# Reordering ScalarE's and VectorE's work between projection and prompt attention, and the last sums and transposes, in a one-layer hybrid decoder step

## The reference

```python
h = rms_norm(x, prm['ln_mix'])
q, kv_c, kv_s, kv_w, gates, z, xbc, dt_raw = split_projection(h, prm['w_in'])
o_cmp, p_cmp = compressed_attention(q, compress_kv(kv_c, *cmp_params(prm)), qpos)
idx = select_blocks(p_cmp, qpos, -(-T // SEL_BLOCK))
# o_sel: attention over the selected blocks; o_win: sliding window of 512
attn = gate_branches(gates, o_cmp, o_sel, o_win)
ssd_y, conv_new, ssm_new = mamba2_mixer(z, xbc, dt_raw, ...)
# finish_layer
x = x + jnp.concatenate([attn, ssd_y], axis=-1) @ prm['w_out']
h = rms_norm(x, prm['ln_mlp'])
x = x + jnp.square(jax.nn.relu(h @ prm['w_up'])) @ prm['w_down']
# at the end
y_prompt = rms_norm(hp, ln_final); y_sample = rms_norm(hs, ln_final)
```

## Time and profile before

| | us |
|---|---|
| median of 3 runs | 2792.65 |
| lowest and highest run | 2785.09, 2793.06 |
| profiled execution, its own time | 2792.96 |
| its span, first to last instruction | 2791.2 |
| TensorE busy in the span | 2647.1 |
| VectorE busy | 1137.0 |
| ScalarE busy | 843.3 |
| mean granted TensorE clock | 0.973 of full speed |

### The profile page before, as it was taken

One profiled execution on the slowest core, in us unless ns is written; L12 is line 12 of the kernel. 1 busy time (PEld: TensorE's weight loads), 2 busy tenths in 40 slices (PEclk: granted clock), 3 DMA queues, 4 the chain that ended last, 5 costly groups with the idle time before them and its releaser, 6 DMA issues.

```text
span 2791.2 us, 50988 instructions
## 1 busy us (share of the span) xinstructions
PE 2647.1 (95%) x21237; PEld 2533.8 (91%) x21237; DVE 1137.0 (41%) x1710; ACT 843.3 (30%) x1360; POOL 107.3 (4%) x116
## 2 busy tenths in 40 slices
PE   7889999999699788999999999999999999999998
PEld 6779999998577557998999999999999999999998
DVE  4432224554676578433333333333333233333333
ACT  3242112223565345322212212222122122221233
POOL 0000000000000041110000000000000000000011
PEclk9999999999799888999999999999999999999999
DMA  5145333233002744322323222222222222222222
GB/s 214 61 159 161 95 93 90 73 101 101 3 31 100 213 128 136 98 91 76 94 89 95 90 90 90 90 90 90 93 95 90 90 90 90 90 90 92 95 90 86
DMA packets 241815, 274.64 MB, mean 98 GB/s; under 512 B 19397, under 2 KB 233811, under 8 KB 237494
## 3 DMA queue, kind: packets, MB, share of 16 engines
q1 hardware_dynamic: 238966, 237.88, 27.3%
q0 software_dynamic: 1728, 33.56, 3.2%
q10 hardware_dynamic: 1040, 2.10, 0.3%
HBM read 261.10 MB, written 20.71 MB: 101 GB/s over the span
## 4 chain that ended last, share of the span: by engine, by line
PE 60%; DVE 2%; ACT 1%; issue 1%; DMA 0%; POOL 0%; ACTq 0%; POOLq 0%; DVEq 0%
PE PS L677 58%; DMA sel_t<-in_cache_kv_sel,idx_s 0%; PE PS L2770 0%; ACT sqr L2683 0%; ACT w_hi L658 0%; PE PS L2357 0%; DVE dec L2084 0%; DVE tmp_s L2327 0%; DVE ys L2330 0%; ACT u_hi L2685 0%; DVE u_lo L2701 0%; PE PS L2276 0%; DVE relu L2696 0%; PE PS L2236 0%; DVE st_s L2316 0%
## 5 line engine op out<-in xcount | busy, mean ns | idle before, releaser
L664 DVE TENSOR_TENSOR w_lo<-w_raw,w_hi 128x1024 fp32r<-128x1024 f32 (+1 forms) x388 | 460.5, 1190 | 1321.3 <-ACT w_hi L658 1320.3
L658 ACT ACTIVATE w_hi<-w_raw 128x1024 fp32r<-128x1024 f32 (+1 forms) x388 | 395.6, 1024 | 1479.9 <-PE PS L677 1478.8
L677 PE MATMUL PS<-h_hi,w_hi 128*128 128x260 f32 x3360 | 675.5, 283 | 8.0 <-DVE h_lo L591 3.6
L677 PE MATMUL PS<-h_lo,w_hi 128*128 128x260 f32 x3360 | 675.2, 282 | 0.0
L677 PE MATMUL PS<-h_hi,w_lo 128*128 128x260 f32 x3360 | 673.9, 282 | 0.0
L677 PEld LDWEIGHTS PS<-h_hi,w_hi 128*128 128x128 f32 x3360 | 516.3, 189 | 9.3 <-DVE h_lo L591 3.7
L677 PEld LDWEIGHTS PS<-h_lo,w_hi 128*128 128x128 f32 x3360 | 519.2, 189 | 0.0
L677 PEld LDWEIGHTS PS<-h_hi,w_lo 128*128 128x128 f32 x3360 | 518.1, 189 | 0.0
L677 PE MATMUL PS<-u_hi,w_hi 128*128 128x260 f32 x2048 | 411.2, 282 | 8.4 <-DVE u_lo L2701 8.4
L677 PE MATMUL PS<-u_lo,w_hi 128*128 128x260 f32 x2048 | 410.5, 282 | 0.0
L677 PE MATMUL PS<-u_hi,w_lo 128*128 128x260 f32 x2048 | 409.9, 281 | 0.0
(11 more groups left out here) (454 smaller groups left out, 2321.4 us busy)
## 6 DMA issues: line engine op xcount, KB each, us to landing
w_raw<-in_w_up SPq DMA_DIRECT2D x256, 256.0 KB, 2.8
w_raw<-in_w_down SPq DMA_DIRECT2D x256, 256.0 KB, 2.9
w_raw<-in_w_in SPq DMA_DIRECT2D x160, 256.0 KB, 2.9
w_raw<-in_w_out SPq DMA_DIRECT2D x64, 256.0 KB, 3.0
out_kv_win_s<-in_state_kv_win SPq DMA_DIRECT2D x8, 1022.0 KB, 7.6
win_t<-in_state_kv_win SPq DMA_DIRECT2D x8, 896.0 KB
xtok<-in_x_prompt SPq DMA_DIRECT2D x4, 1024.0 KB, 8.1
st_s<-in_state_ssm SPq DMA_DIRECT2D x8, 512.0 KB, 4.9
```

What stands on the lines that cost most here:

```text
L658: ins = e.activation(hi, raw, ACT.Copy)
L664: ins = e.tensor_tensor(lo, raw, hi.bitcast(F32), ALU.subtract)
L677: mm = e.matmul(PS[:, bank + 2 * m + h, 0:HN], w, x[:, k0 + k, h * HN:h * HN + HN], start=st and c == 0, stop=sp and c == 2)
```

## The change

On ScalarE and VectorE, `segments` is done ahead of the row copies. ScalarE's order becomes: items 0 to 3, the gates, items 4 and 5, the second halves of the compression, item 6, SiLU, item 7, the compressed keys' high half, items 8 to 11, the first two score copies, items 12 to 15. VectorE's becomes: items 0 to 5, the sums of the compression, item 6, the biases, the compressed keys' low half, item 7, the sample queries, items 8 to 11, then `shifted(0)`, items 12 and 13, `shifted(1)`, items 14 and 15, `shifted(2)`, `shifted(3)`. `pc_normed` of group 0 moves from the end of `att_cmp_dve` to behind the first `row_max` of attention. The programs of TensorE, GpSimd and SP are the same there.

At the end, GpSimd adds up the squares of 14 tiles and VectorE those of the last two. TensorE has four fills, whose tiles are all among the first 12, ahead of the ten sums. The fills come in another order, and the sample rows are written out third instead of last.

```diff
         def rows_act(e):
+            e.wait_ge(g_out, G_IN)
+            segments(e, 1, lambda a, b: e.activation(a, b, ACT.Copy), p_seg_a)
             rows_copy(e, 0, lambda a, b: e.activation(a, b, ACT.Copy), r_act)
-            segments(e, 1, lambda a, b: e.activation(a, b, ACT.Copy), p_seg_a)
...
+            segments(e, 0, lambda a, b: e.tensor_copy(a, b), p_seg_d)
             rows_copy(e, 1, lambda a, b: e.tensor_copy(a, b), r_dve)
-            segments(e, 0, lambda a, b: e.tensor_copy(a, b), p_seg_d)
...
                              ACT.Copy).then_inc(p_half.sem, 1)
+            stack_act(e, 6, 7)
             for c in range(2):
                 e.wait_ge(*p_sum(c + 1))
...
                              bias=bias1[:, c:c + 1]).then_inc(p_silu.sem, 1)
+            stack_act(e, 7, 8)
             kcp_high(e)
...
+            stack_dve(e, 6, 7)
             e.wait_ge(*p_w2(1))
...
             kcp_low(e)
+            stack_dve(e, 7, 8)
...
             e.wait_ge(*a_gate(1))
-            for g in range(NKV):
+
+            for g, n in ((0, 12), (1, 14), (2, 16)):
+                stack_dve(e, 8 if g == 0 else n - 2, n)
                 shifted(g)
-            pc_normed(e, ch, 0)
+            shifted(3)
...
+            stack_act(e, 8, 12)
             scores_out(0)
             scores_out(1)
-            stack_act(e, 8, len(STACKED))
+            stack_act(e, 12, len(STACKED))
...
             row_max(0)
+            pc_normed(e, ch, 0)
             for u in range(NU):
...
-            for k in range(KT):
+            for k in range(KT - 2):
                 e.wait_ge(o_sq, KT + k + 1)
...
-        Y_FILLS = [(t, q) for t in range(5) for q in range(4)]
+        Y_FILLS = [(0, 0), (0, 1), (0, 2), (1, 0), (0, 3), (1, 3), (1, 1), (1, 2)]
+        Y_FILLS += [(t, q) for t in (4, 2, 3) for q in range(4)]
+        Y_FIRST = 4
...
+            e.wait_ge(y_0rdy, KT - 2)
+            e.wait_ge(g_out, G_LAST + KT - 2)
+            for f in range(Y_FIRST):
+                fill(f)
+            e.wait_ge(g_out, G_LAST + KT)
+            e.wait_ge(o_sum, 2 * KT - 2)
+            e.wait_ge(o_sum_d, 2)
+            for t in range(5):
+                n = P if t < 4 else NB
+                last = e.matmul(PS[0:n, 7, t:t + 1], ssq_a[:, y_src(t)], ones[:, 0:1], start=True, stop=True)
+            last.then_inc(y_rs, 1)
+            e.wait_ge(y_0rdy, KT)
+            for f in range(Y_FIRST, len(Y_FILLS)):
+                fill(f)
...
         def final_dve(e):
+            e.wait_ge(o_sum, 2 * KT - 2)
+            for k in range(2):
+                e.wait_ge(o_sq, 2 * KT - 1 + k)
+                if k:
+                    e.wait_ge(o_sum_d, 1)
+                e.tensor_tensor(ssq_a[:], ssq_a[:], sq2[:, k, :], ALU.add).then_inc(o_sum_d, 1)
             e.wait_ge(y_col, 2)
...
-            for t in range(5):
-                e.wait_ge(y_ev_a, 2 * (t + 1))
-                e.wait_ge(y_ev_d, 2 * (t + 1))
+            for t in (0, 1, 4, 2, 3):
+                e.wait_ge(y_ev_a, y_done(t, 3)[0])
+                e.wait_ge(y_ev_d, y_done(t, 3)[1])
...
             rows_act(e)
-            stack_act(e, 0, 8)
+            stack_act(e, 0, 4)
             gate_act(e)
+            stack_act(e, 4, 6)
             cmp_p_act(e)
...
             rows_dve(e, ch)
-            stack_dve(e, 0, 8)
+            stack_dve(e, 0, 6)
             cmp_p_dve(e)
-            stack_dve(e, 8, len(STACKED))
             q_dve(e, ch)
```

More of the change, by code:

```diff
@@ L2749, in build_program, with y_done @@
         y_rms, y_rstd = small[:, 32:37], small[:, 40:45]
-        Y_FILLS = [(t, q) for t in range(5) for q in range(4)]
+        Y_FILLS = [(0, 0), (0, 1), (0, 2), (1, 0), (0, 3), (1, 3), (1, 1), (1, 2)]
+        Y_FILLS += [(t, q) for t in (4, 2, 3) for q in range(4)]
+        Y_FIRST = 4
+        def y_done(t, q):
+            f = max(Y_FILLS.index((t, x)) for x in range(q + 1))
+            return f // 2 + 1, (f + 1) // 2
         def y_src(t):
@@ L2757, in final_pe, with fill @@
         def final_pe(e):
-            e.wait_ge(g_out, G_LAST + KT)
-            e.wait_ge(o_sum, 2 * KT)
-            for t in range(5):
[L2761 to L2765, removed]
+            def fill(f):
+                t, q = Y_FILLS[f]
                 n = P if t < 4 else NB
@@ L2789, in build_program @@
         y_ready = sem("y_ready")
+        o_sum_d = sem("o_sum_d")
         def final_dve(e):
+            e.wait_ge(o_sum, 2 * KT - 2)
[4 more added lines that the diff above has]
+                e.tensor_tensor(ssq_a[:], ssq_a[:], sq2[:, k, :], ALU.add).then_inc(o_sum_d, 1)
             e.wait_ge(y_col, 2)
```

## The result

The changed kernel takes 2775.01 us (median of 4 runs, 2774.18 to 2775.95) against 2791.07 for the kernel before (2785.09 to 2793.06). The ratio is 0.9936, with a 95% interval of 0.9923 to 0.9948: 16 us by the medians, 14.5 to 21.5 us by the interval. The forecast was 2776.5 and 16.2 us. The profiled execution took 2774.28 us, its span 2772.6.

The account below looks back on a forecast made before the run. TensorE, busy 95% of the span, was taken as the bound, with output writing bounding the end. Gains of 12.7 us before attention and 3.5 us at the end summed to 16.2 us, giving 2776.5 us; range 2769 to 2784.

Parts of the forecast that it names:

- ScalarE's chain to SiLU: Before the compressed scores: segments ahead of row copies and ScalarE's new order start SiLU 5.4 us sooner, near 696.2.
- The moved key block: Behind SiLU: the moved block could delay the compressed keys' high half; cost between 0 and 0.4 us, taken as 0.
- VectorE in one piece: Compressed scores to first attention score: VectorE's work, 22.1 us without waits, puts that score at 722.1, 13.9 us sooner.
- Both margins: Before attention: ScalarE's lead over VectorE, 0.75 us for key blocks made under a shift, 4 us for query activations.
- The first unit: Start of attention: normalisation of group 0 behind the first row maxima delays the factors; loss 1.25 us, bounds 0 and 2.1.
- one coupled loop: Attention units: the reason given for taking the normalisation's loss as 1.25 us.
- The end: Program's end: VectorE's sums and early fills bring the first output issue to 2774.8, 3.5 us sooner; the end follows whole.
- the later tiles are ready ahead of the writes: Output writing: writes take 2.4 us each against four evictions on two engines, so the end follows the first issue.
- The low clock in the tail: Rival at the end: TensorE's clock falls in the gap anyway, gain 2.6 instead of 3.5 us, time 2777.4; chance 0.09.
- New hand-over waits: Rival before attention: 1.35 us at each of four engine alternations, 5.4 us go, time 2781.9; chance 0.14.
- Absorbed later: Rival behind the first place: the stage's gain is lost later, only the tail counts, time 2789.1; chance 0.09.
- Slower by the clock in attention: Rival in attention: TensorE at half clock makes the change slower by over 0.3%, 2826 us at most; chance 0.03.

Follow-up runs that it names:

- run with the rows first: Changed kernel with the row copies ahead of the segments again, on ScalarE and VectorE; 2780.37 us, ratio 0.9958.
- run without the alternation: Changed kernel with items 8 to 15 in one piece again, on VectorE ahead of all four shifts; 2784.27 us, ratio 0.9968.
- the end alone: Kernel before with only the changed end of the program; ratio 0.9978.
- first-place run: Changed kernel with the end of the program as in the kernel before; 2780.01 us, ratio 0.9954.
- the run with the split write: Changed kernel with the first 128 prompt rows written in two halves, the first as soon as two fills are copied out; 2774.75 us, ratio 0.9934.

## Why the prediction was right

**ScalarE's chain to SiLU.** The query activations were forecast 9.2 us behind the first row transpose and came at 9.4; SiLU 22.2, measured 22.3. The run with the rows first confirms the 2.6 us of the segments.

**The moved key block.** I bounded its cost by 0 and 0.4 and took 0. The high half of the compressed keys did start later (2.01 us behind SiLU instead of 1.58), and the scores did not (3.65 instead of 3.64). The cover named fits the rows: VectorE ends the value bias at 696.97, when the first part of the high half is already there, as it was before.

**VectorE in one piece.** Forecast 22.3 us from the first compressed score to the first attention score, measured 22.43. Both margins held: no bracket on VectorE. The run without the alternation shows the price of losing them.

**The first unit.** Forecast a loss of 1.25, measured 1.17, of which 0.7 to 1.1 are left at the end of attention. That a VectorE step costs the same anywhere in the units would have been wrong: inside unit 0 it costs 0.1 up to the second unit's factors. The forecast did not need that claim, but its reason, "one coupled loop", is too coarse.

**The end.** First issue forecast 7.2 us behind the last residual, measured 7.13; VectorE's sums 0.70 each as taken; products 1.15 against 1.1. After it 13.2, where I had 12.9: the writes took 0.3 us more, in every run with the new end (13.1 to 13.3). The step that was wrong is "the later tiles are ready ahead of the writes". In all twelve profiled executions with the new end the rate drops in the seventh microsecond behind the first issue (to 221 GB/s in the changed kernel, to 0 with the end alone), in the two with the old end it does not (418 and 410). The third tile of prompt rows comes too late for it. That this makes the whole 0.3 us is not shown: the break is longer with the end alone, and the distance there is no longer.

**The low clock in the tail.** This term was mis-sized. I gave it 0.9 us (a gain of 2.6 instead of 3.5) and a chance of 0.09. The clock fell in four of ten executions with these products, but only 0.40 to 0.47 us after the first of them had begun, and cost 0.42. The rule cited from the Trainium skill ("TensorE: Matmul & The Clock Gate", "Part 1: The HAM clock gate") fits: the same instructions behind the same gap of 1.69 us ran either way.

**The rivals.** New hand-over waits: between ScalarE and VectorE there are two of more than 2 us (VectorE 2.28 before item 4's low half, ScalarE 2.19 before item 14). Neither engine's next step on the path came later for it: ScalarE goes on up to SiLU through the first, and VectorE has no bracket behind the second. Absorbed later: nothing of the kind shows in the first-place run, within the scatter of those stages. Slower by the clock in attention: the granted clock over attention was 0.98 before and after.

**What stays open.** 1.86 us of the profile's difference lie before any changed code, and the stages behind attention scatter (below). That the median landed 1.5 us from the forecast is partly luck; that the changed stretches gave 15.8 of the forecast 16.2 us (15.4 where the clock falls in the tail) is not. The limit of 1.25 us that I set on the distance from first score to first weight product of the output projection was too fine: that distance grew by 0.04 us in the changed kernel and by 3.2 in the run with the split write, over the same instructions. For the run with the end alone, the interval starts at 3.4 us where the distances give 2.8; this too was not settled.

## What to carry to other kernels

When two engines make the two halves of an operand, look at the bracket before each half: the second engine's idle time names the instruction that ought to move, and a step that it can do meanwhile (here a shift of 2.05 us over a 1.30 us pair) hides the hand-over. Cost a moved step by what is queued behind it on every engine, not by its length: the same normalisation cost 1.2 us between maxima and factors, and 0.1 us inside a unit. When a step in a coupled loop seems to cost several microseconds, look first whether the wait that is blamed stands in the other version too, and what the clock was in both. At an end bound by output writes the time of the first write counts most, and after it that the next ones never run dry. A wait that asks for all of a group (four shifts, four fills) is worth splitting.

## What was not expected of the hardware

Stages with unchanged instructions differ from execution to execution with TensorE's clock. From the end of attention to the first product of the output projection it took 199.5 to 209.1 us. Here are three whole windows of that stretch, first of the run with the normalisation in unit 0, then of the changed kernel, then of the run with items 8 to 15 in one piece:

```profile
884.25:1083.79 199.54, 161.29 (x1188) 116.73 (x1189) 136.84 (x261) 88.57 (x223) 46.58 (x34) 0.87 0.58 172
```

```profile
879.35:1081.58 202.23, 166.37 (x1188) 117.91 (x1189) 136.76 (x261) 88.24 (x223) 46.82 (x34) 0.84 0.58 170
```

```profile
888.85:1097.98 209.13, 177.57 (x1188) 126.65 (x1189) 137.88 (x261) 88.63 (x223) 46.86 (x34) 0.80 0.56 164
```

The same 1188 products, with mean granted clocks of 0.87, 0.84 and 0.80, and with TensorE busy for 161, 166 and 178 us. VectorE's and ScalarE's busy times agree within 1.2 us. That the clock causes the difference is read from these rows alone; no run forced it. It is several times the size of most steps studied here, so that such a step has to be read from distances inside the trace. Attention has a smaller spread of the kind: five profiled executions with the changed kernel's attention end it 158.8 to 158.9 us behind the first score, the one with items 8 to 15 in one piece 158.5, and the one with the split write 160.4.
